# A two-block transformer on one core: fourteen of 22 up pairs as seven block products instead of thirteen, with the steps around them moved

## What is computed

```python
mixed = (sigmoid(g_a) * y_a + sigmoid(g_b) * y_b) @ w_out          # "wout", the last projection
h = h + rms_norm(mixed, g[1])
xn = rms_norm(h, g[2])
u = causal_depthwise_conv(xn @ w_up, conv_w, conv_b)               # "up", 1024 -> 2 * 2816, three taps
u_gate, u_val = split(u, 2)
ffn = (gelu(u_gate) * u_val) @ w_down                              # "down", 2816 -> 1024
h = h + rms_norm(ffn, g[3])
```

## Time and profile before

| | |
|---|---|
| median of 3 runs | 1509.6 us (1508.28 to 1511.03) |
| the profiled execution | 1509.57 us |
| its span, first to last instruction | 1507.7 us |
| mean granted TensorE clock | 0.994 of full |
| PE, DVE, ACT busy | 97%, 72%, 49% |
| DMA | 185.25 MB, mean 123 GB/s |

### The profile page before, as it was taken

One profiled execution on the slowest core, in us unless ns is written; L12 is line 12 of the kernel. 1 busy time (PEld: TensorE's weight loads), 2 busy tenths in 40 slices (PEclk: granted clock), 3 DMA queues, 4 the chain that ended last, 5 costly groups with the idle time before them and its releaser, 6 DMA issues.

```text
span 1507.7 us, 27986 instructions
## 1 busy us (share of the span) xinstructions
PE 1457.4 (97%) x11573; PEld 1281.0 (85%) x11573; DVE 1092.2 (72%) x1556; ACT 731.8 (49%) x1203; POOL 23.3 (2%) x20
## 2 busy tenths in 40 slices
PE   8999999999998999999999899999989999999998
PEld 7988778889998999999777667767667999998876
DVE  5556557885676889988785785776778889885444
ACT  5343443433334446766344455446546555554343
POOL 0000000000000000000000020000000000000000
PEclk9999999999999999999999999999999999999999
DMA  5155114544681225564765122111113233322322
GB/s 188 57 205 214 71 62 143 161 150 179 244 335 57 84 78 164 182 191 149 224 201 177 60 74 71 57 35 32 40 42 113 85 112 113 112 99 84 98 84 84
DMA packets 49230, 185.25 MB, mean 123 GB/s; under 512 B 5456, under 2 KB 5712, under 8 KB 37712
## 3 DMA queue, kind: packets, MB, share of 16 engines
q1 hardware_dynamic: 47952, 181.30, 35.6%
q10 hardware_dynamic: 1152, 2.16, 0.4%
HBM read 167.71 MB, written 15.73 MB: 122 GB/s over the span
## 4 chain that ended last, share of the span: by engine, by line
PE 78%; DVE 12%; ACT 6%; issue 3%; DMA 1%; POOL 0%; ACTq 0%; DVEq 0%
PE ps L740 15%; PE ps L742 14%; PE ps L741 14%; PE ps L1721 4%; PE ps L1720 4%; PE ps L1719 4%; PE ps L1251 3%; PE ps L1253 3%; PE ps L1252 3%; DVE t L2585 2%; ACT t L1770 2%; PE ps L776 1%; PE ps L777 1%; PE ps L778 1%; PE ps L1425 1%
## 5 line engine op out<-in xcount | busy, mean ns | idle before, releaser
L740 PE MATMUL ps<-t 128*128 128x258 f32 (+3 forms) x1728 | 565.3, 327 | 17.2 <-DVE t L2585 4.2
L742 PE MATMUL ps<-t 128*128 128x258 f32 (+3 forms) x1728 | 554.3, 321 | 0.0
L741 PE MATMUL ps<-t 128*128 128x258 f32 (+3 forms) x1728 | 553.7, 320 | 0.0
L740 PEld LDWEIGHTS ps<-t 128*128 128x128 f32 x1728 | 326.5, 189 | 62.2 <-issue 18.1
L742 PEld LDWEIGHTS ps<-t 128*128 128x128 f32 x1728 | 326.0, 189 | 26.3
L741 PEld LDWEIGHTS ps<-t 128*128 128x128 f32 x1728 | 326.6, 189 | 23.2
L2585 DVE TENSOR_TENSOR t<-t 128x1024 fp32r<-128x1024 f32 (+2 forms) x107 | 175.8, 1643 | 165.1 <-ACT t L1770 164.9
L1770 ACT ACTIVATE t<-t 128x1024 fp32r<-128x1024 f32 (+2 forms) x107 | 148.8, 1390 | 152.9 <-PE ps L742 144.8
L1719 PE MATMUL ps<-t 128*128 128x256 f32 x504 | 140.6, 279 | 0.1
L1721 PE MATMUL ps<-t 128*128 128x256 f32 x504 | 140.5, 279 | 0.0
L1720 PE MATMUL ps<-t 128*128 128x256 f32 x504 | 140.5, 279 | 0.0
(11 more groups left out here) (349 smaller groups left out, 2212.2 us busy)
## 6 DMA issues: line engine op xcount, KB each, us to landing
t<-in_W SPq DMA_DIRECT2D x74, 1024.0 KB, 4.9
t<-in_W SPq DMA_DIRECT2D x74, 512.0 KB, 3.6
t<-in_W SPq DMA_DIRECT2D x115, 256.0 KB, 3.5
up_sums<-t SPq DMA_DIRECT2D x13, 1024.0 KB, 5.0
t<-up_sums SPq DMA_DIRECT2D x28, 256.0 KB, 4.8
t<-up_sums SPq DMA_DIRECT2D x12, 512.0 KB, 5.5
t<-in_W SPq DMA_DIRECT2D x4, 644.0 KB, 3.8
t<-in_XT ACTq DMA_DIRECT2D x8, 264.0 KB, 7.5
```

Of the source, the lines that this page charges most:

```text
L740: pe.matmul(out, wh, xh, start=first, stop=False)
L741: pe.matmul(out, wh, xl, start=False, stop=False)
L742: return pe.matmul(out, wl, xh, start=False, stop=last)
```

## The change

- `PLAIN_UP` is 8 instead of 9, so 14 pairs go as seven products, and the buffer places of the products shift by half.
- One more weight sum. The wout loop makes sums 8 and 9 in chunk 0, 10 and 11 in chunk 1 (10 alone before), 12 and 13 in chunk 2 (11 and 12 before); SP's list stores 10 and 11, then 12 and 13.
- Between the plain and the fast pairs: on ACT `turn_high(2)`, `up_high(0, 3)` and `turn_high(3)` stand ahead of the last plain gelu; on DVE `turn_low(0)` and `(1)` come after tile 14 instead of 15, and `up_low(0, 2)`, `turn_low(2)`, `up_low(0, 3)`, `turn_low(3)` all come ahead of the last plain taps.
- 16 matmuls of 512 columns, whose result nobody reads, behind the norm's spread and ahead of the first up tile.
- After down, ACT's `root` and DVE's reciprocal come ahead of the split of kq's first half.

```diff
--- before.py
+++ after.py
@@ -116,7 +116,7 @@
 
 PLAIN_BANKS = (1, 2, 5, 6, 0, 3, 5, 6)
 
-PLAIN_UP = 9
+PLAIN_UP = 8
 FAST_UP = 22 - PLAIN_UP
 UP0 = AT["up", PLAIN_UP]
 
@@ -673,7 +673,7 @@
                 if n == 24:
                     sums_load(5)
                     sums_load(6)
-                for i in {26: (5,), 27: (6,), 28: (7,), 31: (8, 9), 32: (10,), 33: (11, 12)}.get(n, ()):
+                for i in {26: (5,), 27: (6,), 28: (7,), 31: (8, 9), 32: (10, 11), 33: (12, 13)}.get(n, ()):
                     sums_store(i)
                     if i + 2 < FAST_UP:
                         sums_load(i + 2)
@@ -818,13 +818,13 @@
                 return ins
 
 
-            def blank_products(widths):
-
-                pe.wait_ge(S["half"], 1)
+            def blank_products(out, x, widths):
+
                 for n in widths:
-                    pe.matmul(bank(6, n), qka[:, 0, 0:P], qka[:, 0, 0:n], start=True, stop=True, skip_group_check=True)
-
-            blank_products((512, 512, 512, 512, 512, 128, 128, 128))
+                    pe.matmul(out[:, 0:n], x[:, 0:P], x[:, 0:n], start=True, stop=True, skip_group_check=True)
+
+            pe.wait_ge(S["half"], 1)
+            blank_products(bank(6, 512), qka[:, 0, 0:512], (512, 512, 512, 512, 512, 128, 128, 128))
 
             H2 = (264, 264)
             w = (whi[:, 0, :].rearrange("p (k c) -> p k c", k=8), wlo[:, 0, :].rearrange("p (k c) -> p k c", k=8))
@@ -1200,6 +1200,7 @@
             norm_sum_of(1, 4, 7)
             norm_spread(1, 4)
             w = weights(AT["up", 0], 8)
+            blank_products(bank(6, 512), mh[:, 0, 0:512], 16 * (512,))
             pe.wait_ge(S["ev_wo_a"], 4)
             pe.wait_ge(S["ev_wo_d"], 4)
             pe.wait_ge(S["rst"], 2)
@@ -2146,10 +2147,10 @@
                 if i == PLAIN_UP - 1:
                     up_keep(0, 0)
                     up_high(0, 2)
+                    turn_high(2)
+                    up_high(0, 3)
+                    turn_high(3)
                 gelu(i)
-            turn_high(2)
-            up_high(0, 3)
-            turn_high(3)
             for f in range(FAST_UP):
                 i, more = PLAIN_UP + f, f + 1 < FAST_UP
                 if f >= 1:
@@ -2199,8 +2200,8 @@
                         square(3, b, bank(b, T2))
                         if b % 2:
                             ac.activation(mo[:, b, 0:T2], bank(b, T2), ACT.Copy).then_inc(S["ev_dn_a"], 1)
+            root(3, 0)
             split_part(AT["kq", 0], 0)
-            root(3, 0)
             spread(3, 0)
             for k in range(8):
                 ac.wait_ge(S["rs_b"], 8 + k + 1)
@@ -2895,12 +2896,12 @@
 
             for c in range(4):
                 split(AT["wout", c] + 1)
-                if c in (0, 2):
-                    up_sums(8 + 3 * c // 2)
+                if c < 3:
+                    up_sums(8 + 2 * c)
                 for i in range(2):
                     j = 2 * c + i
                     if i == 1 and c < 3:
-                        up_sums((9, 10, 12)[c])
+                        up_sums(9 + 2 * c)
                     if j % 2 == 0:
                         dv.wait_ge(S["mm_wout"], j + 1)
                         dv.tensor_copy(halves(mo[:, j, 0:TQ]), pair(0, TQ // 2)).then_inc(S["ev_wo_d"], 1)
@@ -3035,7 +3036,7 @@
                 if j in (11, 13):
                     turn_sum(j - 11)
                     turn_sum(j - 10)
-                if j == 15:
+                if j == 14:
                     turn_low(0)
                     turn_low(1)
             for f in range(FAST_UP):
@@ -3043,14 +3044,13 @@
                 if f >= 1:
                     up_gather(f - 1, 1)
                     up_low(f, 3)
-                taps(2 * i - 1)
                 if f == 0:
                     up_low(0, 2)
                     turn_low(2)
                     up_low(0, 3)
+                    turn_low(3)
+                taps(2 * i - 1)
                 gated(i - 1)
-                if f == 0:
-                    turn_low(3)
                 if more:
                     up_low(f + 1, 0)
                     up_low(f + 1, 1)
@@ -3093,7 +3093,6 @@
                 add(3, b)
             for b in (4, 6):
                 dv.tensor_copy(mo[:, b, 0:T2], bank(b, T2)).then_inc(S["ev_dn_d"], 1)
-            split_part(AT["kq", 0], 0)
 
             def xm_low(k):
 
@@ -3103,6 +3102,7 @@
 
             dv.wait_ge(S["eps"], 4)
             dv.reciprocal(rcol[:, 0:4], rcol[:, 0:4]).then_inc(S["pow"], 1)
+            split_part(AT["kq", 0], 0)
             dv.wait_ge(S["rst"], 4)
             for k in range(8):
                 dv.scalar_tensor_tensor(out=mo[:, k, 0:T2], in0=mo[:, k, 0:T2], scalar=V("g3", k), in1=rst[:, 0:T2],
```

## The result

The changed kernel takes 1512.71 us (median of 21 runs, 1511.25 to 1513.83), the kernel before on the same chip 1510.62 us (21 runs, 1508.28 to 1511.32): ratio 1.0016, with a 95% interval from 1.0009 to 1.0022. It is slower, by 0.16% or 2.1 us, where 0.7 us faster was forecast, and its median lies above the end of the range (1512.2). The profiled execution took 1511.65 us.

A forecast was written before the change was run, and what follows sets the result against it. The prediction took TensorE (PE), busy 97% of the span, to bound the kernel. Its terms, -1.4 + 1.0 + 1.0 + 0 - 1.3 + 0 = -0.7 us, took 1509.57 to 1508.9 us, range 1505.2 to 1512.2.

The forecast's parts named there:

- The fourteenth sum: Wout and its norm: one more weight sum with its load and store makes split_up1 late; +1.0 us, 0 to +2.1.
- The transition: From plain to fast pairs: DVE takes up the last plain tile 0.9 us late; +1.0 us, from -1.44 to +2.0.
- The pair: Up stage: one more pair made as seven products takes 10.13 us instead of 11.53; -1.4 us.
- Rival B: Norm after wout: sum 13's store lands late, split_up1 starts at 453 or after; +1.5 us, 1511.1, chance 0.20.
- Blank products: Ahead of the first up tile: 16 products fit the 3.85 us gap but DVE paces the tile; 0, at most +0.7.
- Rival C: First up tile: the clock is the bound and the blank products win back 2.5 us; 1506.4, chance 0.06.
- A: Rival at the transition: the stall before product 4 goes, sums' stores stay hidden; -4.1 us, 1505.5, chance 0.17.
- D: Rival in the fast pairs: the fourteenth is paced by DVE or ACT and saves nothing; 1510.3, chance 0.05.
- Norm after down: After down: root and reciprocal ahead of the split start the spread 1.06 us earlier; -1.3 us, -0.9 to -1.6.
- Start of down: Down's first block loads later, after the products' last low split, but stays hidden; 0, to +0.7 us.
- The sum: Whole kernel: all terms together, -1.4 + 1.0 + 1.0 + 0 - 1.3 + 0 = -0.7 us, giving 1508.9.

The follow-up runs named there:

- g2: f1 with the z tiles, turned sums and turn_low(0) spread otherwise over the plain pairs; ratio to the kernel before 0.9989.
- h1: g2 with turn_high(1) on ACT moved from between the last two first taps to before them; 1507.41 us against 1509.89 for the kernel before, ratio 0.9990.
- f2: Changed kernel with z tiles, their parts, turned sums and turn_high one pair sooner on ACT and DVE; ratio to the kernel before 1.0023.
- f1: Changed kernel with the loads of weight sums 10 to 13 issued ahead of the stores of 8 to 11; ratio to the kernel before 1.0003.
- i2: Changed kernel measured once more without an edit, on another chip; ratio to the kernel before 1.0006.
- e4: e3 with weight sum 8 ahead of filling tile 30, and its store and the load of sum 10 issued there; ratio to the kernel before 1.0009.
- e2: Changed kernel with ten blank products of 512 columns on a free bank ahead of product 4; ratio to the kernel before 1.0010.
- e1: Changed kernel with up_keep(0, 1) moved up on ACT to right behind turn_high(2); ratio to the kernel before 1.0014.
- f3: Changed kernel with the edits of f1 and f2 together; ratio to the kernel before 1.0013.
- e3: Changed kernel with the even tile's copy and `add` ahead of each weight sum on DVE in wout; ratio to the kernel before 1.0034.
- f4: Changed kernel without the sixteen blank products behind the norm's spread; ratio to the kernel before 1.0016.
- g3: g2 with the order of ACT and DVE at the transition as in the kernel before; ratio to the kernel before 0.9989.
- g1: Changed kernel back at 13 pairs, keeping only the blank products and the new order around the norm after down; ratio to the kernel before 0.9981.
- h2: h1 with up_keep(0, 1) right behind turn_high(2) on ACT; ratio to the kernel before 0.9994.

## Why the prediction was wrong, step by step

Two terms of the sum failed, both for what a delay sets off. The fourteenth sum was to delay PE's even tiles of wout by 0.1 us, and took 1.7. The transition was to cost 1.0 us, worked out at the full clock, and cost 2.6, of which 1.5 is the low clock behind the stall.

- **The pair** (-1.4): right. 14 fast pairs run at 10.11 us with no gap but those of the transition: 11.53 - 10.11 = 1.42.
- **The transition** (+1.0, to +2.0): the mechanism right, the size wrong, measured +2.6 and once +3.8. The walk gave the last plain tile taken up 0.9 us late and a gap of 2.4; the trace has 561.89, 1.1 us behind the tile's end, and 2.56, with product 4 2.7 us late where the 1.6 of the earlier trace rows (578.57 - 571.20 - 5.78) and the forecast 1.0 make 2.6. The term that was left out is the clock. I had checked it around the norms, where the profile shows it at 0.50, but priced the longer stall here as if PE came back at full speed, because it does so after the 1.44 us of the earlier trace rows. g2 and h1 price that: 0.92 us of gap, 1.7 us of time. The 0.1 us given to the second pair is 0.57 in f2 and h1, where the tile is on time, and 0 in the changed kernel, whose first pair is itself later.
- **The fourteenth sum** (+1.0): right in sign, 2.0 measured, and the wrong sub-term carried it. The reciprocal was to be 0.9 us late behind `split_up1`; it was 0.28. The 0.1 us for the copies behind sums 10 and 12 was 1.7: the rows at 429.39 and 442.16 mark 1.20 us, but two pairs of tiles of 11.53 us each take 12.06 and 12.77 (417.33 to 429.39 to 442.16), 1.77 over. I had followed the stores to their last user and not the loads to their first: sum 10's load stood at 0.80 us late already in the earlier trace rows, and each sum added puts every later load further back. That PE's last tile "comes no earlier" was true, and it came later. The list of gaps at the head of the prediction counts five and leaves several of the same timeline out, among them the 0.58 us at 418.65, the kernel before's own stall on the copy of an even tile: the kind that grew. And the prediction's last sentence names what happened, sum 12 waiting so long that tile 6 stands (it does, at 442.16), but no term of the sum prices it. Rival B took the store for the thing that decides; f1 shows the loads. It was nearest in time (1511.1), and its far end named "later evacuations stopping PE too" without a price. Its mechanism is real, and smaller: the store did not hold `split_up1` in the first profiled execution (it began at 451.71, right behind its table load), but it did for 0.52 us in i2, where A and B lost 3.3 us and not 2.0, and for 0.92 in e4. The late loads come first in that chain too, as the last store waits for sum 13.
- **Blank products** (0): right; the same 30.94 us with and without. Rival C falls, and so do A (product 4 did not come sooner) and D (the pair saves its 1.42). The Trainium skill's rule against idle gaps ("TensorE: Matmul & The Clock Gate", Why this matters for your kernels) is worth nothing at the place where the change follows it, and 0.9 us (e2) at the transition, where it doesn't.
- **Norm after down** (-1.3, from -0.9 to -1.6): right in sign, -1.75 here, which is past the far end of its range (-1.6), and -0.6 to -2.0 by the spread of E in the runs. The 1.06 us came as worked out (1.08 by the gaps, 1.70 and 0.62), and the spread ran whole at the full clock (1.16 us for 1.85), of which I had counted half. That second part is luck of the execution: in e1, f1, f2 and g2 the spread took 2.07 or 2.08 us.
- **Start of down** (0): right. PE has no gap at the start of down, and 6.5 us in one of 0.69 us in both kernels; from the last product to the column sums 130.84 and 130.83 us.
- **The sum.** -1.4 + 1.0 + 1.0 - 1.3 was -0.7; -1.42 + 2.86 (D and the last plain pairs) + 2.0 - 1.75 is +1.7. Three terms passed or came near their bounds: the transition (2.6 for at most 2.0), the sum (2.0 for at most 2.1) and, the other way, the norm. Its surplus of 0.45 us hid a part of the miss. The transition went past by a second effect of a delay that was itself well forecast; the sum reached its bound by a wait that had 0.1 us.

## What to carry to other kernels

A delay handed to a full engine has two prices: the stall, and what the clock takes behind it; work out the second wherever a stall grows, from the rows at either level. When a stage gets one more load and store in a queue, follow the load to its user first, and look whether it stands behind a store that it doesn't need: there issuing the loads ahead was worth 2.0 us, and the added bytes cost nothing. When a stage gives up one unit of cover, the side work in it needs new places on each engine that takes part; one operand left at its old place on ACT cost 1.7 us.

## What the runs showed that I had not expected

- One stretch of code ran at two paces, 293.9 to 294.0 us in seven profiled executions and 295.7 to 295.9 in eleven, each of the two kernels in both groups, at a granted clock of 1.00; the starts of its matmuls of 256 columns in the 18 pairs stood 0.1167 us apart on average in the one and 0.1178 in the other. What makes it is open. It is as large as the whole effect of the change.
- A marked gap understates a stall: 0.24 and 0.96 marked in wout, 0.53 and 1.24 lost; 2.56 marked at product 4, and its start 2.69 late. The mark counts from the end of the matmul before, 0.28 us behind its start by the rows, where the next usually starts after 0.12.
- In the up stage each stall of PE of 2.27 to 2.58 us (f2 and f3 near 517; the changed kernel twice, e3, e4, f1, f4, g2 and g3 at product 4) was followed by a granted clock of 0.50, and none of those of 1.44 to 1.54 (the kernel before twice, g1, h1, e1, h2, f2 and f3). After the same gap of 2.56 us the changed kernel's fast pairs lost 4.3 us in one execution and 5.5 in the other, where the clock stayed low for longer.
